# Two transformer blocks on one core: one reciprocal square root in retention, an earlier start of its values, and modulation's products and sums moved forward

## What is computed

```python
mx = jnp.split(silu_c @ w_mod[l] + b_mod[l], 6, axis=-1)      # modulation
...
s_new = s * c_dec + jnp.einsum('bhcd,bhce->bhde', kb * k_dec, vb)
a = jnp.einsum('bhid,bhjd->bhij', qb, kb) * intra
y = jnp.einsum('bhij,bhje->bhie', a, vb) + jnp.einsum('bhid,bhde->bhie', qb, s) * q_dec
...
mu = jnp.mean(y, axis=-1, keepdims=True)
var = jnp.mean((y - mu) ** 2, axis=-1, keepdims=True)
yn = ((y - mu) * lax.rsqrt(var + EPS)) * gn_g
out = jax.nn.silu(gate) * yn
```

## Time and profile before

| | us |
|---|---|
| median of 3 runs | 2638.38 (2637.64 to 2640.54) |
| profiled execution, its own time | 2646.84 |
| its span | 2645.1 |
| TensorE busy | 2487.2 (94%) |
| VectorE busy | 1344.5 (51%) |
| ScalarE busy | 861.9 (33%) |
| mean granted TensorE clock | 0.977 |

### The profile page before, as it was taken

The page is one execution under the profiler, slowest core; times in us unless marked ns, Lnnn a source line. Parts: engine busy times, 40 slices in busy tenths (PEclk is TensorE's granted clock), DMA queues, the critical chain, the costliest instruction groups (busy, mean ns, idle before and its releaser), DMA issues. The chain is left out here.

```text
span 2645.1 us, 35585 instructions
## 1 busy us (share of the span) xinstructions
PE 2487.2 (94%) x15034; PEld 1934.9 (73%) x15034; DVE 1344.5 (51%) x2152; ACT 861.9 (33%) x1370; POOL 261.7 (10%) x249
## 2 busy tenths in 40 slices
PE   6999989999999999999899999898988999998977
PEld 4888657888888888897679999674743578873333
DVE  4323554666667413433647777437666766432223
ACT  3324333333234212334444434214331653330001
POOL 0500120000000100301200000000031110012112
PEclk8999979999999999999999999899999999999999
DMA  6113731111111122124512222420200114359997
GB/s 252 64 57 118 261 113 48 49 64 64 64 64 49 55 66 70 66 78 153 203 48 95 82 96 82 152 94 25 81 32 9 49 48 144 143 201 368 421 421 321
DMA packets 56671, 322.36 MB, mean 122 GB/s; under 512 B 8061, under 2 KB 14205, under 8 KB 24573
## 3 DMA queue, kind: packets, MB, share of 16 engines
q1 hardware_dynamic: 44798, 300.27, 30.8%
q0 software_dynamic: 5696, 12.59, 1.2%
q10 hardware_dynamic: 6016, 7.18, 0.8%
HBM read 315.82 MB, written 12.58 MB: 124 GB/s over the span
## 5 line engine op out<-in xcount | busy, mean ns | idle before, releaser
L1000 PE MATMUL ps<-work_rounded,ring_rounded 128*128 128x512 f32 (+1 forms) x2016 | 530.4, 351 | 11.2 <-DVE work_rounded L398 5.9
L1000 PE MATMUL ps<-xn_rounded,ring_rounded 128*128 128x512 f32 (+2 forms) x2304 | 540.0, 346 | 0.0
L2150 PE MATMUL ps<-xn_rounded,ring_rounded 128*128 128x258 f32 (+2 forms) x2816 | 531.7, 311 | 0.0
L2150 PEld LDWEIGHTS ps<-xn_rounded,ring_rounded 128*128 128x128 f32 x2816 | 411.8, 189 | 30.9
L1000 PEld LDWEIGHTS ps<-xn_rounded,ring_rounded 128*128 128x128 f32 x2304 | 371.7, 190 | 57.4 <-issue 0.5
L1000 PEld LDWEIGHTS ps<-work_rounded,ring_rounded 128*128 128x128 f32 x2016 | 331.2, 189 | 68.8 <-DVE work_rounded L398 9.8
L1000 PE MATMUL ps<-big_rounded,ring_rounded 128*128 128x512 f32 (+1 forms) x1200 | 319.5, 356 | 15.2 <-DVE big_rounded L900 8.8
L900 DVE TENSOR_TENSOR ring_rounded<-ring,ring_rounded 128x2048 fp32r<-128x2048 f32 (+4 forms) x107 | 192.1, 1796 | 257.2 <-ACT ring_rounded L864 256.9
L2150 PE MATMUL ps<-work_rounded,ring_rounded 128*128 128x256 f32 (+1 forms) x1232 | 278.5, 307 | 1.8 <-PEq L807 1.8
L864 ACT ACTIVATE ring_rounded<-ring 128x2048 fp32r<-128x2048 f32 (+4 forms) x107 | 160.9, 1505 | 290.0 <-PE ps L1000 269.8
L1000 PEld LDWEIGHTS ps<-big_rounded,ring_rounded 128*128 128x128 f32 x1200 | 197.0, 190 | 56.5 <-DVE big_rounded L900 9.9
(11 more groups left out here) (437 smaller groups left out, 3137.5 us busy)
## 6 DMA issues: line engine op xcount, KB each, us to landing
ring<-in_stream SPq DMA_DIRECT2D x141, 1024.0 KB, 4.8
big<-in_experts SPq DMA_DIRECT2D x44, 1024.0 KB, 26.8
ring<-in_stream SPq DMA_DIRECT2D x32, 704.0 KB, 4.0
ring<-in_experts SPq DMA_DIRECT2D x22, 1024.0 KB, 27.5
xn<-in_experts SPq DMA_DIRECT2D x15, 1024.0 KB, 28.4
work<-in_experts SPq DMA_DIRECT2D x15, 1024.0 KB, 28.0
big<-in_first_modulation SPq DMA_DIRECT2D x8, 1024.0 KB, 14.2
work<-in_bias ACTq DMA_DIRECT2D x20, 256.0 KB, 4.2
```

The lines of the kernel that those rows point to most:

```text
L1000: mm = pe.matmul(out[:, a - u.first:b - u.first], lhs, rhs, start=j == 0 and n == 0 and not u.onto, stop=j == terms - 1 and n == len(passe ...
L2150: mm = pe.matmul(out[:, a:b], ws[:, k, :], x[k][:, a - base:b - base], start=k == 0 and n == 0, stop=k == KT - 1 and n == 2)
```

## The change

- In `attention`, `share` is rounded up instead of down: context attention's eight products lie in units 0, 1, 3, 4, 6, 7, 9 and 10 instead of 1, 2, 4, 5, 7, 8, 10 and 11.
- At the end of context attention TensorE gets two idle matmuls of 256 columns; at the end of layer 1's neighbourhood attention two of 512 columns.
- In both attentions VectorE does modulation's `finish` before it stores the last output tile, not after.
- Retention's first pair starts the part within the chunk when three of the five state steps are carried, and waits for all five before the context's chunks (layer 0) and before the part from the states.
- Retention's root is one activation (`Abs_reciprocal_sqrt`) instead of a logarithm and an exponential. One small activation of that function comes right after the strip's high half; the small logarithm that stood between the pairs goes.
- `normalise` gets a second wait for the same root, ahead of its other two. The order in which VectorE stores the last pair and normalises the first is not altered by any line of the diff.

```diff
--- before.py
+++ after.py
@@ -1102,7 +1102,7 @@
         tpsum = [self.bank(b, width) for b in turn_banks]
         opsum = [self.bank(b) for b in out_banks]
 
-        share = [range(u * modulation.count // units, (u + 1) * modulation.count // units) if modulation else () for u in range(units)]
+        share = [range(-(-u * modulation.count // units), -(-(u + 1) * modulation.count // units)) if modulation else () for u in range(units)]
         squared, summed = self.sig("squared"), self.sig("summed")
         views = self.split_ahead(ahead)
         strip_pieces = [(n, value[:, a:z], high[:, a:z]) for n, value, high in views for a, z in pieces(value.shape[1])]
@@ -1189,6 +1189,8 @@
                 values(units // group - 1)
                 if normed_pairs:
                     sum_pair(heads // 2 - 1)
+                if modulation:
+                    self.keep_multiplying(pe, spsum[0], 2)
 
             @block.sync
             def _(sp):
@@ -1237,9 +1239,9 @@
                         if u == at_unit + 1:
                             dve.wait_ge(next_high.sem, next_high.at(n + 1))
                             self.split_low(dve, value, high)
-                store(units // span - 1)
                 if modulation:
                     modulation.finish(dve)
+                store(units // span - 1)
 
             @block.scalar
             def _(act):
@@ -1562,6 +1564,8 @@
                 if modulation:
                     modulation.sum(pe)
                 values(units - 1)
+                if not need_ctx:
+                    self.keep_multiplying(pe, sps[0][1], 2)
 
             @block.sync
             def _(sp):
@@ -1653,9 +1657,9 @@
                     for a, b in pool_runs:
                         ins = dve.tensor_scalar(px[:, n, a:b], pooled[n][:, a:b], self.v(("pool_scale", l), n), None, ALU.mult)
                     ins.then_inc(pool_evicted.up(), 1)
-                store(2)
                 if modulation:
                     modulation.finish(dve)
+                store(2)
 
             @block.scalar
             def _(act):
@@ -1759,7 +1763,7 @@
         turned, decayed, updated = self.sig("turned"), self.sig("keys_decayed"), self.sig("state_updates")
         carried, queried = self.sig("states_carried"), self.sig("queries_decayed")
         weighed, valued, stored = self.sig("weighed"), self.sig("valued"), self.sig("stored")
-        squared, varied, logged, rooted, gated = self.sig("squared"), self.sig("varied"), self.sig("logged"), self.sig("rooted"), self.sig("gated")
+        squared, varied, rooted, gated = self.sig("squared"), self.sig("varied"), self.sig("rooted"), self.sig("gated")
         half = [slice(0, 64), slice(64, 128)]
 
         def update(c, d, p):
@@ -1815,21 +1819,25 @@
 
                 def values(p):
                     pe.wait_ge(weighed.sem, weighed.at(2 * (p + 1)))
-                    if p == 0:
-                        pe.wait_ge(carried.sem, carried.at(5))
-                    if p >= 2:
+                    if p < 2:
+                        pe.wait_ge(carried.sem, carried.at((3, 5)[p]))
+                    else:
                         pe.wait_ge(stored.sem, stored.at(p - 1))
 
                     def out(c, hh):
                         return yps[p % 2][half[hh], c * P:(c + 1) * P] if c < 4 else ycps[half[hh], (c - 4) * P:(c - 3) * P]
 
                     for c, a in chunks:
+                        if c == 4 and p == 0:
+                            pe.wait_ge(carried.sem, carried.at(5))
                         if c == 4 and p >= 1:
                             pe.wait_ge(stored.sem, stored.at(p))
                         for hh in range(2):
                             h = 2 * p + hh
                             pe.matmul(out(c, hh), vr[:, c, h * 64:(h + 1) * 64], aw[p % 2][hh][:, a:a + P], start=c in (0, 4), stop=False)
                     pe.wait_ge(queried.sem, queried.at(p + 1))
+                    if p == 0:
+                        pe.wait_ge(carried.sem, carried.at(5))
                     for c, a in chunks:
                         for d in range(2):
                             if (c, d) in ((4, 0), (5, 1)):
@@ -1845,7 +1853,7 @@
 
                     pe.wait_ge(squared.sem, squared.at(p + 1))
                     if p == 1:
-                        pe.wait_ge(logged.sem, logged.at(1))
+                        pe.wait_ge(rooted.sem, rooted.at(1))
                     else:
                         pe.wait_ge(weighed.sem, weighed.at(6))
                     for a, b in pieces(qw):
@@ -1888,25 +1896,18 @@
                         act.wait_ge(varied.sem, varied.at(1))
                     act.activation(sq[p % 2][:, 0:qw], px[:, RQ + p, 0:qw], ACT.Square).then_inc(squared.up(), 1)
 
-                def logarithm(p):
+                def root(p):
                     act.wait_ge(varied.sem, varied.at(p + 1))
                     if p >= 2:
                         act.wait_ge(gated.sem, gated.at(1))
-                    act.activation(rstd[p % 2][:, 0:qw], var[p], ACT.Ln, bias=EPS).then_inc(logged.up(), 1)
-
-                def root(p):
-                    act.wait_ge(logged.sem, logged.at(p + 1))
-                    act.activation(rstd[p % 2][:, 0:qw], rstd[p % 2][:, 0:qw], ACT.Exp, scale=-0.5).then_inc(rooted.up(), 1)
+                    act.activation(rstd[p % 2][:, 0:qw], var[p], ACT.Abs_reciprocal_sqrt, bias=EPS).then_inc(rooted.up(), 1)
 
                 self.high_ahead(act, views)
+                act.activation(self.small[:, 124:125], self.ones[:, 0:1], ACT.Abs_reciprocal_sqrt)
                 square(0)
                 square(1)
-                logarithm(0)
                 root(0)
-                act.activation(self.small[:, 124:125], self.ones[:, 0:1], ACT.Ln)
                 square(2)
-                logarithm(1)
-                logarithm(2)
                 root(1)
                 root(2)
 
@@ -1988,6 +1989,7 @@
 
                 def normalise(p):
                     t = px[:, RQ + p, 0:qw]
+                    dve.wait_ge(rooted.sem, rooted.at(p + 1))
                     dve.wait_ge(vstep.sem, vstep.at(p + 1))
                     dve.wait_ge(rooted.sem, rooted.at(p + 1))
                     dve.tensor_tensor(t, t, rstd[p % 2][:, 0:qw], ALU.mult).then_inc(gated.up(), 1)
```

## The result

The changed kernel takes 2621.2 us (2620.0 to 2621.5, 4 runs) against 2638.4 us before (2637.6 to 2640.5, 4 runs): a ratio of 0.9933, with a 95% interval of 0.9915 to 0.9950. That is 17.2 us less, well clear of the 0.2% that can be told from nothing. The forecast was 2608.5 with a range of 2602.5 to 2622.5, so the time lies 1.3 us inside the upper end.

A forecast was written before the change was run, and what follows sets the result against it. TensorE, busy 94%, was taken as the bound, so only its idle, needless or lower-clock time could be won. Terms summed to 30.0 us: 2638.4 - 30.0 = 2608.4, say 2608.5; range 2602.5 to 2622.5 for 8 in 10.

The forecast's parts named there:

- (a): Context attention falls to 1.2 GHz anyway; that part gives 2.4 us, time 2621.5; chance 0.17.
- (b): Clock falls in retention's tails and values, idle matmuls become the bound; 11 us lost, time 2619.5; chance 0.08.
- signs of being wrong: Context attention's clock at 0.50, a strip ending TensorE's waits there, or other stages changing by more than a few us.
- Context attention: Product 0 fills the entry gap, clock stays at 2.4 GHz, retention starts at 344.8 instead of 360.4: 15.6 us.
- the same offset: Whole kernel: timed median assumed 8.5 us under the profiled time after the change, as before it.
- rival (d): Whole change gives under 5.3 us: moved waits met by others, no lost clock in timed runs; 2635; chance 0.03.
- Layer 0's retention: Stage in layer 0 shortens from 45.0 to 37.7 us by start 0.5, early values 2.5 and roots 4.3.
- The values' early start: Retention's first pair starts values before all state steps end: 2.5 us in layer 0, 3.6 in layer 1.
- The roots: Retention's tail: one activation per root, fewer table loads, idle matmuls end last; 4.3 us in layer 0, 2.6 in layer 1.
- Layer 1's retention: Stage in layer 1 shortens by 7.5 us: held clock 1.3, early values 3.6, roots 2.6.
- The border to it: Border into layer 1's retention waits for two idle matmuls of 512 columns, 0.45 us later than before.
- Rival (c): Latent attention in the second block sticks at the lower clock; 43 us lost, time 2651.5; chance 0.03.

The follow-up runs named there:

- attentions alone: Kernel before with all the diff's changes in the two attentions and none of those in retention; 2631.8 us, ratio 0.9962.
- roots back: Changed kernel with logarithm and exponential in place of the one root activation, and the small logarithm between; 2627.4 us, ratio 0.9943.
- retention-only kernel: Kernel before with the changed retention and the attentions of before; 2626.9 us, ratio 0.9940.
- run without idle matmuls: Changed kernel without the idle matmuls at the ends of context attention and layer 1's neighbourhood attention; 2619.3 us, ratio 0.9919.

## Why the prediction was right, and where its size was off

The sign and the mechanisms were right and the time is inside the range, near its upper end; the point was 12.7 us too low. That it is inside is luck in part. The upper end of 2622.5 was put there to take in rivals (a) and (b), and neither happened; the forecast's own 2604 to 2613, which had 0.69, was missed. Two of its signs of being wrong came up, in small: a strip ended a wait of TensorE in context attention (0.92 us), and the stages behind changed by 2.6 us. The other signs came as forecast: context attention at full clock and over at 346.9, the retentions at 37.3 and 31.3 us (37.7 and 31.6), and no load between squares and roots.

- **Context attention** was priced at 15.6 us. Against the profile it was worked out from, it is 14.2 (41.0 to 26.8): the clock held, and what is missing is the strip's 0.92 us, which the text had as "with 7.1 the last waits 1 us". It counted on 4.9 us from issue to landing, read where the clock was low; at full clock the products ask for strips sooner, and in this stage they took 4.7 to 7.5, median 6.6. The idle matmuls that "end with VectorE's store and cost nothing" cost some 0.6 us, as the run without them shows. That the 0.75 us left would do no harm was taken from other gaps under 1 us; it came out so in every profile of the changed attentions, but the rule behind it did not hold at a border (0.87 us).
- **The term that was mis-sized** for the timed runs is this same one, by "The median lies 8.5 us under the profiled time ... so I put the same offset under it". The 8.5 us were not an offset but the very thing that the largest term counted: 24 us more at the lower clock in one profiled execution than in the usual one, which made the stage 10.6 us longer (41.0 and 30.4). Against a usual run this term is 3.6 us, 12 less than forecast. The text met the truth in rival (d), "the timed runs have no lost clock to give back", gave it 3 in 100 and tied it to a gain of nearly nothing, instead of taking the 15.6 alone away: 2608.5 and 12 are 2620.5, and 2621.2 was measured. Rival (a) comes to 2621.5, but by another way: its clock would fall in the changed kernel too, and it does not.
- **Layer 0's retention**: 7.3 forecast, 7.7 and 8.2 against the two profiles. The split was wrong. The values' early start gives 0.95 us, not 2.5, and that is the 16 records at full clock: the forecast had them at the lower clock (1.8) and added 0.7 for a clock that the rest of the change holds anyway. VectorE's store(0) is held by the strip's low half, as was said (it starts 20.3 us into the stage with the early start and without), and the second pair, whose values start 0.97 us sooner, makes that up, as was said too. The roots give 3.5, not 4.3. The start, put at 0.5, gives 0.9. The run of the attentions alone took 3.9 us off this stage without touching it, all through the clock: against the second profile of before 1.4 us up to the first pair's values, 2.0 from there to the last averages, 0.4 in the tail. The idle matmuls account for the 0.9 at the start; the rest is falls that came in the one profile and not in the other.
- **Layer 1's retention**: 7.5 forecast, 7.5 and 7.6 measured. The attentions alone give 1.4 to 1.5 (1.3 forecast), and retention's two parts the other 6.1 (6.2 forecast). Each part alone is worth 2.3 or 2.4; taken away last, the values' start costs 3.7 (3.6 forecast) and the roots 3.8 (2.6 forecast), for falls come or stay away with either. The close agreement of the sum is luck in part.
- **The border to it** comes 0.62 us later, 0.45 forecast; "the clock should hold" because of the idle matmuls is not so in layer 1, where it held without them; `finish` ahead of the store did it, as far as one profile each can tell.
- **Roots**: the new function takes 0.81 us at 768 columns and 0.58 to 0.60 at 512, the logarithm's time, with one load behind the strip's high half and none between squares and roots. That the loads would leave the way to the border and "the idle matmuls are next" was right: these end 7.0 us behind the last values and VectorE 5.5 (7.1 and 5.4 forecast), and halving them gave 1.2 and 1.7 us of the 1.5 and 2.0 that its expectation named. The Trainium skill's rule that `ln` then `exp` need one load ("ScalarE: Activation LUTs", section on table sets) stays contradicted by the run with the roots back, which has a load of 1.28 us between them again.
- **The sum** has a term of 0.1 us that no sentence of the prediction works out, and no run shows it; it changes nothing.
- **"What is behind these stages ... only moves"** was off by 2.6 us, which the changed kernel takes longer there (1301.5 to 1304.1; its repeat 1303.4) though nothing in it is altered. In these two profiles 1.4 us of it go at the entry of latent attention and 2.0 behind it, less 0.8 won on the way there. Windows at both places show the clock. Of before, again:

```profile
2034.00:2042.00 8.00, 7.06 (x21) 4.02 (x22) 1.95 (x4) 1.96 (x4) 1.28 (x1) 0.79 0.00 0
2137.00:2141.00 4.00, 4.00 (x19) 3.23 (x18) 3.96 (x5) 1.37 (x3) 0.00 (x0) 1.00 0.01 4
```

and of the changed kernel, the same work:

```profile
2014.00:2022.00 8.00, 7.37 (x17) 4.24 (x18) 1.63 (x3) 1.19 (x2) 1.27 (x1) 0.57 0.00 1
2117.00:2121.00 4.00, 4.00 (x13) 3.14 (x12) 3.96 (x3) 0.33 (x1) 0.00 (x0) 0.62 0.01 4
```

At the same gaps the clock is down for longer. In the changed kernel's second profile it is not (0.79 and 1.00 at both places, as in before), and yet this stretch is long there too; these two falls are no property of the change. Over all profiles the stretch takes 1301.0 to 1304.1 us, and the one between the two retentions 899.0 to 902.3. What puts an execution at one end of that was not tried. Rival (c), a clock that sticks low through latent attention, appeared in none.

## What to carry to other kernels

Ask of a profiled execution whether it is the usual one before a term is drawn from it: its time 8 us above the timed runs, beside a stretch at the lower clock, was the sign, and a second profile of the unchanged kernel settled it. Put work that must be done anyway into the gap ahead of a start that waits for other engines, rather than idle matmuls; here both held the clock, but the work also freed its buffer, so that loads were issued sooner. When a tail gets shorter, look again at the idle matmuls that once filled it: here they had become the end of the stage.

## What the runs showed of the hardware that was not expected

- One program, with the same 2.35 us of idle time ahead of it, stayed at 1.2 GHz for 30.7 us in one execution (TensorE never idle in them) and for 6.8 us in another; the retention-only kernel had 13.7. In the changed kernel the same kinds of instructions, with the products one unit earlier, held 2.4 GHz to the stage's end.
- The length of a gap is not enough to tell a fall. 2.38 us of idle time in layer 0's tail brought the clock down in the kernel before and not in the run with the roots back or in that of the attentions alone. 2.12 us ahead of the second scores of layer 0's retention did so in the run of the attentions alone (24 records in 2.83 us) and not in the changed kernel (1.61). At layer 0's border 0.87 us were enough in the run without idle matmuls, while 1.13 us at layer 1's in the same run had no fall behind them.
